# Dealing the filling work of a recurrence anew: three gate products to a step, projections product by product, and a scan two steps sooner

## The reference

```
h = adaLN(rmsnorm(x));  z = h @ w_in          # q, f_fw, f_bw, v, g, xr, xg and the merge gates
# mixer A, per head (4), per direction (2), in chunks of 32 tokens
S_t = diag(f_t) S_{t-1} + k_t v_t^T;  o_t = S_t^T q_t
y_a = (rmsnorm(o) * silu(g)) @ w_branch_a
# mixer B, per direction (2): a gated linear recurrence over a short convolution xc of xr
r = sigmoid(xc @ w_r + b_r);  i = sigmoid(xc @ w_i + b_i)      # blocks of 64 channels
a = exp(log_a(r));  h_t = a_t h_{t-1} + sqrt(1 - a_t^2) (i_t * xc_t)
y_b = ((h_fw + h_bw) * gelu(xg)) @ w_branch_b
x = x + g1 * ((sigmoid(ga) * y_a + sigmoid(gb) * y_b) @ w_out)
x = x + g2 * peer(adaLN(rmsnorm(x)))          # top-16 product keys, 128 gathered experts per token
```

## Time and profile before

| | us |
|---|---|
| median of 3 runs | 3947.18 (3942.33 to 3949.27) |
| the profiled execution, its own time | 3947.58 |
| its span | 3945.8 |
| PE busy | 2948.1 (75%) |
| DVE busy | 2783.8 (71%) |
| POOL busy | 1305.9 (33%) |
| ACT busy | 676.5 (17%) |

### The profile page before, as it was taken

One profiled execution on the slowest core, in us unless ns is written; L12 is line 12 of the kernel. 1 busy time (PEld: TensorE's weight loads), 2 busy tenths in 40 slices (PEclk: granted clock), 3 DMA queues, 4 the chain that ended last, 5 costly groups with the idle time before them and its releaser, 6 DMA issues.

```text
span 3945.8 us, 46322 instructions
## 1 busy us (share of the span) xinstructions
PE 2948.1 (75%) x16906; PEld 1323.5 (34%) x16906; DVE 2783.8 (71%) x6805; ACT 676.5 (17%) x1391; POOL 1305.9 (33%) x1174
## 2 busy tenths in 40 slices
PE   8999999988799997856666666666656666665555
PEld 3665665545444442212322222212212222221111
DVE  4545546766787786747888768877877786887555
ACT  2534533011122120000111111110111111101000
POOL 0000000014443443433444434444444444444443
PEclk9999999989999998988888778778977788887777
DMA  4010003579999999999999999999999999999998
GB/s 184 24 35 26 24 25 149 184 255 409 416 414 411 415 402 418 417 422 411 404 399 414 414 408 411 417 404 419 415 412 411 410 415 408 414 415 411 420 417 338
DMA packets 214040, 1343.26 MB, mean 340 GB/s; under 512 B 24722, under 2 KB 45714, under 8 KB 62898
## 3 DMA queue, kind: packets, MB, share of 16 engines
q0 software_dynamic: 165888, 1208.03, 74.6%
q1 hardware_dynamic: 46628, 129.65, 8.8%
q10 hardware_dynamic: 1296, 2.62, 0.2%
HBM read 1326.55 MB, written 13.67 MB: 340 GB/s over the span
## 4 chain that ended last, share of the span: by engine, by line
DMA 37%; PE 36%; DVE 13%; issue 10%; POOL 3%; ACT 1%; POOLq 0%; SPq 0%; DVEq 0%; ACTq 0%
DMA arena<-in_uv,mask_b 13%; PE ps L794 12%; DMA arena<-in_uv,ones 11%; DMA arena<-in_uv,mask_f 11%; PE ps L1472 10%; DVE arena L1313 4%; PE ps L659 3%; PE ps L772 3%; POOL arena L628 3%; DVE arena L1193 2%; PE ps L1466 2%; PE ps L690 1%; PE ps L723 1%; DVE arena L1153 1%; PE ps L1524 1%
## 5 line engine op out<-in xcount | busy, mean ns | idle before, releaser
L794 PE MATMUL ps<-arena 64*64 64x512 f32 x9216 | 1458.8, 760 | 937.4 <-DVE arena L1193 925.5
L1313 DVE CUSTOM_DVE_ANT_0 arena<-arena 128x1024 f32<-128x1024 f32 x1152 | 1410.9, 1225 | 737.0 <-DMA arena<-in_uv,mask_b 286.8
L794 PEld LDWEIGHTS ps<-arena 64*64 64x64 f32 x9216 | 351.2, 158 | 1885.7 <-DVE arena L1193 1374.1
L628 POOL DMA_INDIRECT arena<-in_uv,ones x384 | 440.7, 1148 | 621.5 <-PE ps L794 480.5
L628 POOL DMA_INDIRECT arena<-in_uv,mask_f x384 | 435.3, 1134 | 591.3 <-PE ps L794 502.9
L628 POOL DMA_INDIRECT arena<-in_uv,mask_b x384 | 424.1, 1104 | 593.9 <-PE ps L794 505.7
L988 ACT ACTIVATE arena<-arena 128x2 f32<-128x2 f32 x576 | 117.1, 203 | 2639.8 <-DVE arena L1313 2570.2
L1472 PE MATMUL ps<-arena 128*128 128x384 f32 x1152 | 384.3, 490 | 1.8 <-DVE arena L1759 1.8
L1193 DVE TENSOR_SCALAR arena<-arena 128x64 f32<-128x64 f32 x1152 | 307.4, 309 | 0.4 <-ACT arena L988 0.3
L772 PE MATMUL ps<-arena 128*128 128x384 f32 x768 | 269.0, 497 | 0.0
L610 POOL IOTA arena<- 128x16 f32 x1 | 0.1, 144 | 804.0 <-PE ps L672 804.0
(11 more groups left out here) (209 smaller groups left out, 2367.7 us busy)
## 6 DMA issues: line engine op xcount, KB each, us to landing
arena<-in_w_mg SPq DMA_DIRECT2D x16, 1536.0 KB, 17.0
arena<-in_w_in SPq DMA_DIRECT2D x28, 512.0 KB, 3.3
arena<-in_w_mod SPq DMA_DIRECT2D x8, 1792.0 KB
arena<-in_w_mod SPq DMA_DIRECT2D x4, 2048.0 KB, 23.4
arena<-in_w_out SPq DMA_DIRECT2D x2, 4096.0 KB, 17.1
arena<-in_w_q SPq DMA_DIRECT2D x8, 1024.0 KB, 15.5
arena<-in_w_q SPq DMA_DIRECT2D x4, 2048.0 KB, 36.2
arena<-in_uv,ones POOLq DMA_INDIRECT x384
```

The costliest lines, as they stand in the source:

```text
L628: nc.gpsimd.indirect_dma_start(out=RG[n % RING], out_offset=None, in_=uv, in_offset=bass.IndirectOffsetOnAxis(ap=EIDX[t % 3][:, s:s + 1], ...
L794: mm = nc.tensor.matmul(PS[c * HALF:(c + 1) * HALF, 2 * r + n, :], DG[rows, s, :], RG[s][rows, D + n * 512:D + (n + 1) * 512], start=(g == ...
L1313: ins = v.tensor_tensor_reduce(u, u, h2, 1.0, 0.0, ALU.mult, ALU.add, PRE[:, s % RING:s % RING + 1])
```

## The change

Gate units go three to a step into steps 0 to 3, in place of two to a step in steps 0 to 5. The 48 products of the late projections are dealt out one by one over steps 4 to 17: four in each of steps 10 to 15 and three in each of the others, so that a chunk of eight can end within a step. ACT takes a chunk out in the step in which it ends (steps 6, 9, 11, 13, 15 and 17, where it was 7, 9, 11, 13, 15 and 17). `decay` moves with `GATE_STEPS` from steps 6, 8 and 10 to steps 4, 6 and 8, and `lru` from steps 12 to 17 to steps 10 to 15 (the call is `lru(it - 1)`). No arithmetic is added or taken away.

```diff
-GATE_STEPS = 6
-LRU_STEP = 11
+GATE_STEPS, GATES_A_STEP = 4, 3
+LRU_STEP = 9
...
+def part_of(it):
+    quota = lambda n: 4 if LRU_STEP < n <= LRU_STEP + 6 else 3
+    first = sum(quota(n) for n in range(GATE_STEPS, it))
+    return first, first + quota(it)
...
-                for swap in range(2):
-                    g, n = divmod(2 * it + swap, NCH)
+                for c in range(GATES_A_STEP * it, GATES_A_STEP * (it + 1)):
+                    swap = c % 2
+                    g, n = divmod(c, NCH)
                     z = z_bank(B_GATES + g, n)
...
-                    c, part = divmod(it - GATE_STEPS, 2)
-                    project(*late_chunk(c), range(part * KD // 2, (part + 1) * KD // 2))
+                    for n in range(*part_of(it)):
+                        project(*late_chunk(n // KD), (n % KD,))
...
-                    for c in range(2 * it, 2 * it + 2):
+                    for c in range(GATES_A_STEP * it, GATES_A_STEP * (it + 1)):
...
-                elif (it - GATE_STEPS) % 2:
-                    b, n = late_chunk((it - GATE_STEPS) // 2)
+                    return
+                lo, hi = part_of(it)
+                for c in range(lo // KD, hi // KD):
+                    b, n = late_chunk(c)
...
-                if d < 0:
+                if not 0 <= d < 2:
                     return
```

More of the change, by code:

```diff
@@ L119, in late_chunk @@
     return (B_G, B_XG)[c // NCH], c % NCH
+def part_of(it):
+    quota = lambda n: 4 if LRU_STEP < n <= LRU_STEP + 6 else 3
+    first = sum(quota(n) for n in range(GATE_STEPS, it))
+    return first, first + quota(it)
+assert part_of(TI - 1)[1] == 2 * NCH * KD
 def wait_alone(eng, sem, value):
```

## The result

The changed kernel took 3967.72 us (3964.89 to 3972.87, 5 runs) against 3945.65 us before (3942.33 to 3949.27, 5 runs): ratio 1.006, interval 1.0049 to 1.0072. The forecast was slower by 11.2 us; it became 22. As a time, 3958.4 was forecast with a range of 3948 to 3966, and 3967.72 lies above it. A second set of runs gave 3962.09 us against 3944.43, ratio 1.0044 (1.003 to 1.0058). The profiled execution took 3965.41 us, its span is 3963.7.

The account below looks back on a forecast made before the run. PE's work bounds product steps, a 3.16 us ring through DVE and ACT the gate steps. Per head 354.73 + 0.36 + 0.1 = 355.19 against 352.39: +2.80, +11.2 for four; from median 3947.18, 3958.4 us, range 3948 to 3966.

Parts of the forecast that it names:

- The bank wait: Gate steps 0 to 3: third unit waits for the first's bank; units to outputs 2.33 or 2.94 us, before 1.50.
- The sum of +11.2 us: Four heads of stage A, each +2.80 us: last step's outputs at 355.19, where before they were at 352.39.
- the small terms: Product steps: ACT's square root in step 6, +0.36 us a head, and the recurrence on DVE, +0.1.
- The square root's step: Step 6: a chunk's taking out and a table load make ket_out 2.28 us late, 1.92 covered, leaving +0.36 a head.
- The recurrence: Six steps of four products: the shorter step ahead makes DVE's copy 0.05 us late; +0.1 a head, at most 0.6.
- The clock falls in the gate steps: Rival, chance 0.03: new waits in the four gate steps halve PE's clock, up to +12 us a head, near 4006.
- nothing in the earlier trace shows a fall, at 83% or above: Argument against a clock fall: head 1's clock was 1.00 before, with PE busy 83% of the gate steps.
- The forecast has 0.72: Chance given to the main forecast of 3958.4 us, whose own range is 3954 to 3963.
- waits of 0.66 and 1.27 us: PE's forecast waits for ACT ahead of third units, in turn over the gate steps.
- The banks don't hold the third unit: Rival, chance 0.07: gate steps stay at 3.16 us, -2.69 us a head, -10.8 in all, 3936.4.
- The drain that the Trainium skill adds to a table load: Step 6, two switches of about 1.38 us each: some 2.8 us more a head, near 3970; left out of the sum.

## Why the prediction was wrong

*The bank wait* was right in mechanism, place and size. Forecast for head 1: outputs of step 3 16.41 us behind the first units; measured 16.5. Steps took 4.61 and 4.03 us (forecast 4.60 and 3.99), steps with three and four products 3.43 and 4.08 as forecast, and from the first outputs to the last it was 65.29 us (65.4). The sum of +11.2 us stands for what it covers: the four bank waits and the small terms measured 11.0.

*The small terms.* The square root's step cost 0.2 us (0.36): the outputs of steps 7 and 8 are 3.63 apart, the others 3.43. The recurrence cost 0.13 (0.1): 4.13 and 4.15 in steps 10 and 11, 4.08 in the others.

*The step that failed* is the clock, which the sum left at 1.00, as a term of nothing, and which had 0.03 as the rival "The clock falls in the gate steps". The argument against it, "nothing in the earlier trace rows shows a fall, at 83% or above", took PE's mean share as the measure, and "The forecast has 0.72" rested on that. I listed waits of 0.66 and 1.27 us for it and left out the longest, which my own sum had: units at 286.60, their work done by 287.48, third unit at 289.03, 1.55 us in step 0. The runs with only that wait removed and only that wait kept show that it is the one, and every fall seen began at its end. The price was wrong as well, in another way: a long fall came in four of twelve scans and cost 10.5 us, not 12 in every head. With four scans an execution that would be some 14 us; by the medians the two sets of runs lie 11.1 and 6.7 us above the 11.0 of the bank waits, about one long fall, and two thirds of one. (The forecast's time stood on a median of 3947.18 for the kernel before; with two more runs it was 3945.65. From that, the same sum gives a time 1.5 us lower.)

What the Trainium skill reports there ("TensorE: Matmul & The Clock Gate", A second HAM failure mode: psum-queue depth-cycling), a clock that swings where PE idles briefly between groups of products that go through PSUM banks in turn, agrees with this trace in kind: 1.00 to 0.50 and back. The difference is that here one wait of 1.56 us in a scan sets it off, in five of twelve scans.

*The rival "The banks don't hold the third unit"* had about the right arithmetic for a kernel that wasn't this one: -10.8 us worked out, -11.3 measured once the bank was there (3932.61 against 3943.94).

The drain that the Trainium skill adds to a table load ("ScalarE: Activation LUTs", What ACT_TABLE_LOAD costs) was rightly left out: the step with two loads took 0.2 us more, where two drains would have made it about 3.

What stays open: why a fall comes in one scan and not in the next, with the same 1.56 us wait, and why some last 27.3 us and others 6.8 or 3.4. That the shorter waits keep the clock down is argued from one fall and the times of one kernel, not shown.

## What to carry to other kernels

Before work is packed more densely between the links of a chain, count the buffers it goes through: with two banks in turn, a third unit in a step waits for the first one's reader, whatever idle time the engines show on average. When you ask what the clock will do, look for PE's longest single wait and not only at its mean share, in every step, the first one too; and read the clock head by head over several executions, since medians alone pointed to the wrong theory here. Where a chain leaves PE idle for a time, fill just that time, as one product of 0.645 us did in 0.62 idle. Here that filler had a bank of its own; without one it wasn't tried.

## What the runs showed of the hardware that was not expected

- One idle stretch of 1.56 us of PE, behind work at full speed, could bring its clock from 2.4 to 1.2 GHz (granted 1.00 to 0.50): in 6 of 16 scans that had it, within 0.4 us of its end. Waits of 0.67 and 1.25 us in turn did not, in four scans.
- The falls lasted 27.3 us (four times), 6.8 and 3.4 us, and cost 10.4 to 10.6, 2.2 and 1.5 us. In the first of the long ones PE had waits and was busy 21.83 of 25.00 us; in that of 6.8 us it was busy 6.00 of 6.00.
- Work that nobody reads, put into the waits, made the kernel 7 and 11 us faster than the two sets of the changed kernel, by medians counted from the kernel before in each set.
- Two gate units on different quarters of the array take 0.88 us together, one alone 0.86. The second gains nothing if its bank comes free late: the same pair then took 1.72.
